# A hybrid DeltaNet and attention layer on one Trainium2 core: the products of levels 1 to 5 of the triangular inverse, one head at a time on half of the array

## The chip, the cores and the metric

One Trainium2 chip, one core of it. The metric is the device time of one execution, in microseconds (us). A result is the median of several executions, and a change is judged by the ratio of two kernels that ran on the same chip.

## The reference, cut to what matters

One residual layer over 4096 frames of width 1024. After an RMS norm and an input projection, two groups of heads work side by side: four heads of gated DeltaNet (head dimension 128, chunks of 64 frames) and eight query heads of sliding-window attention. Both are gated, concatenated and mapped by an output projection. The change lies in the DeltaNet part, in the solve of a unit lower triangular system for each head and chunk:

```python
lower = jnp.where(strict, jnp.einsum('bhnid,bhnjd->bhnij', k_beta, kc) * decay, 0.0)
eye = jnp.eye(CHUNK, dtype=jnp.float32)
rhs = jnp.concatenate([v_beta, k_beta * jnp.exp(G)[..., None]], axis=-1)
sol = lax.linalg.triangular_solve(eye + lower, rhs, left_side=True, lower=True, unit_diagonal=True)
```

The solved values feed a recurrence over the chunks, `v_new = val - kcu @ state`, from which output and next state follow.

## The kernel before, in words

The sequence is cut into 32 tiles of 128 frames. The kernel has 33 steps. Step `t` projects tile `t` and, in the same step, does all the work of the heads and the output projection for tile `m = t - 1`. The first step has only the projection, the last only the other part, and 31 steps have both. Each engine runs its own list of instructions, in the order in which `step` writes it, and the engines meet at semaphores (`done` waits for one).

PE's order is written out by hand (`step`, L383). The projection of tile `t` is cut into pieces, and `fill(n)` (L387) puts `n` of them between two parts of the other work, so that PE has something to do while DVE and ACT handle what the part before left. A piece is 24 or more matmuls in f16: lines L402 and L409. L597 is the output projection.

The inverse: the kernel solves for a tile of 128 frames at once. For each of the four heads it builds the inverse of a 128x128 unit triangular matrix by doubling. Level `lv` (1 to 6) joins diagonal blocks of size `2**lv` in pairs. With T the inverse so far, M the matrix, it takes P, the product of the odd rows' part of M with the even columns of T, keeps what belongs to the block pairs (a mask), and subtracts the product of the odd blocks of T with that from T. Only half of the columns of T and of M are touched at each level, 64 of each head's 128. The kernel keeps these halves packed: `t_even(lv)` and `t_odd(lv)` (L295, L298) are 128x256 each, 64 columns for each of the four heads, in one of two buffers `t_buf`; `m_odd` (L144) is the same for M, packed by POOL (`pack_m`, L1261).

A level from 1 to 5 has these parts:

- PE, `level_p` (L421): waits for T of the level before (`t_ready` from DVE, `t_moved` from ACT) and for `m_odd_ready`. It then multiplies pairs of heads: `m_odd` (128 columns, two heads) against `t_even` (128 columns, the same two heads), f32, into `bank[2]`, columns 0 to 255: line L432, two products. Each 128x128 result holds four 64x64 blocks, one pair of heads against itself and across. Then two transposes of `t_odd` into `bank[3]`, columns 0 to 255: line L436.
- DVE, `couple` (L947): reads both results, multiplies them by the level's mask and writes `below` (128x256): line L953, one operation of 256 columns. The mask of the level also clears the blocks across heads.
- ACT, `copy_u` (L694): copies the transposes to `u_odd` (L699), and `t_odd` to its place in the next level's packing (`next_columns(lv, 1)`, L700).
- PE, `level_t` (L447): waits for `p_ready` and `u_ready`, multiplies `u_odd` against `below` for the two pairs of heads, f32, into `bank[2]`, columns 256 to 511: line L452, two products.
- DVE, `update` (L956): subtracts the result from `t_even` and writes the next level's packing: line L958, one operation of 256 columns.

Level 6 is another form (L440, L444, L457): four products of 64 result rows, one for each head, and four transposes. Between the levels stand other parts of the step: the transposes of the softmax (L552), the attention's product with its values (L565: weights of 128 rows by 64 columns, results in turn on partitions 0 to 63 and 64 to 127), the product of keys and state (L417), and a fill. L531 is the attention's scores (weights of 64x64, on all four quarters of the array in turn), L518 four transposes ahead of the inverse. Of the work of a level, PE's order is: `level_p`, other parts or none, `fill(1)`, `level_t`, `fill(1)`. `level_p(4)` comes right after L565; ahead of every other `level_p` and `level_t` stands a fill, L409 for levels 1 to 3 and L402 for levels 4 (`level_t`) and 5.

On DVE the parts of the inverse stand between a convolution (L870, L872), the softmax (L1041, L1052), the gates and L1068, which scales the right-hand sides. The masks are made once, at the start: `mask_sym` from PE's transposes (L818), then five sums (L821).

Of the kernel before, what the change touches and what calls it, by code (L numbers as in the profile page):

```python
# [25 lines left out]
ALU = mybir.AluOpType  # L26
# [13 lines left out]
LEVELS = 7  # L40
# [34 lines left out]
def build(nc, x, pre_norm_w, w_in, conv_w, dn_a_log, dn_dt_bias, dn_out_norm_w, sw_sinks, w_out,  # L75
# [8 lines left out]
    with ExitStack() as ctx:  # L84
# [9 lines left out]
        bank = [ctx.enter_context(nc.psum_tensor(f"bank{i}", [128, 512], F32)) for i in range(8)]  # L94
# [45 lines left out]
        u_odd, below = flat[:, 0:256], flat[:, 768:1024]  # L140
        t_nat = work[:, 2:6, :]
        unread = prod.rearrange("p h n -> p (h n)").bitcast(mybir.dt.bfloat16)
        t_buf = [inv_t[:, :, :].rearrange("p h n -> p (h n)"), flat[:, 256:768]]
        m_odd = [cw[:, :, :].rearrange("p h n -> p (h n)")[:, 256 * i:256 * i + 256] for i in range(2)]  # L144
# [13 lines left out]
        masks = sb("masks", [128, LEVELS, 128], F16)  # L158
# [8 lines left out]
        def cut(at, n):  # L167
# [59 lines left out]
        p_turn, p_ready, tp_turn, t_turned, t_ready, u_ready, t_moved, m_odd_ready = (  # L227
            {lv: Nth(s, hi - lo + 1, lv - lo) for lv in range(lo, hi + 1)} for s, lo, hi in (
                (sem("p_turn"), 1, 6), (sem("p_ready"), 1, 6),
                (sem("tp_turn"), 1, 5), (sem("t_turned"), 1, 6), (sem("t_ready"), 1, 5),  # L230
                (sem("u_ready"), 1, 6), (sem("t_moved"), 1, 5), (sem("m_odd_ready"), 1, 5)))

        mask_turned, mask_link = sem("mask_turned"), sem("mask_link")
# [31 lines left out]
        def over_heads(ap, h):  # L265

            return ap.unsqueeze(1).broadcast_to([128, h, ap.shape[1]])
# [14 lines left out]
        def columns(flat_ap, lv):  # L282

            if lv == LEVELS - 2:
                return flat_ap.rearrange("p (q r) -> p q r", r=2 ** lv)
            return flat_ap.rearrange("p (q s r) -> p q s r", s=2, r=2 ** lv)

        def next_columns(lv, which):

            m = 2 ** lv  # L290
            if lv == LEVELS - 2:
                return t_nat.rearrange("p h (b s r) -> p (h b) s r", s=2, r=m)[:, :, which, :]
            return t_buf[lv % 2].rearrange("p (s q w r) -> p q s w r", s=2, w=2, r=m)[:, :, :, which, :]

        def t_even(lv):  # L295
            return t_buf[(lv - 1) % 2][:, 0:256]
# [4 lines left out]
        def heads(b):  # L301
            return bank[b][:, :].rearrange("p (h n) -> p h n", h=4)
# [58 lines left out]
        def _(pe):  # L361
            mm = nc.tensor.matmul
# [3 lines left out]
            for lv in range(LEVELS - 2):  # L366
                last = nc.tensor.transpose(mask_t[:, lv, :], masks[:, lv, :], ident16)
# [15 lines left out]
            def step(t, p, mix, proj, prep):  # L383
                m = t - 1
# [36 lines left out]
                def level_p(lv):  # L421

                    if lv == 1:
                        done(pe, t0_ready, m)
                    else:
                        done(pe, t_ready[lv - 1], m)
                        done(pe, t_moved[lv - 1], m)
                    if lv < LEVELS - 1:
                        done(pe, m_odd_ready[lv], m)
                        for g in range(2):  # L430
                            at = slice(128 * g, 128 * g + 128)
                            last = mm(bank[2][:, at], m_odd[lv % 2][:, at], t_even(lv)[:, at], start=True, stop=True)  # L432
                        last.then_inc(p_turn[lv].sem, 1)
                        for g in range(2):
                            at = slice(128 * g, 128 * g + 128)
                            last = nc.tensor.transpose(bank[3][:, at], t_odd(lv)[:, at], ident)  # L436
                        last.then_inc(t_turned[lv].sem, 1)
                        return
                    for h in range(4):
                        last = mm(bank[2][64:128, 64 * h:64 * h + 64], mt[:, h, 64:128], t_nat[:, h, 0:64],  # L440
                                  start=True, stop=True)
                    last.then_inc(p_turn[lv].sem, 1)
                    for h in range(4):
                        last = nc.tensor.transpose(heads(3)[:, h, :], t_nat[:, h, :], ident)  # L444
                    last.then_inc(t_turned[lv].sem, 1)

                def level_t(lv):  # L447
                    done(pe, p_ready[lv], m)
                    done(pe, u_ready[lv], m)
                    if lv < LEVELS - 1:  # L450
                        for g in range(2):
                            last = mm(bank[2][:, 256 + 128 * g:384 + 128 * g], u_odd[:, 128 * g:128 * g + 128],  # L452
                                      below[:, 128 * g:128 * g + 128], start=True, stop=True)
                        last.then_inc(tp_turn[lv].sem, 1)
                    else:
                        for h in range(4):
                            last = mm(bank[3][0:64, 64 * h:64 * h + 64], below[:, 64 * h:64 * h + 64],  # L457
                                      inv_u[:, h, 64:128], start=True, stop=True)
                        last.then_inc(up_turn, 1)
# [16 lines left out]
                for h in range(4):  # L476
                    last = nc.tensor.transpose(heads(2)[:, h, :], g_cols[:, h:h + 1].broadcast_to([128, 128]), ident)
# [5 lines left out]
                for h in range(4):  # L483
                    last = nc.tensor.transpose(heads(6)[:, h, :], k4[:, h, :], ident)
                last.then_inc(k_turned, 1)
                done(pe, qkv_ready[2], m)
                for h in range(4):
                    last = nc.tensor.transpose(heads(7)[:, h, :], v4[:, h, :], ident)
# [8 lines left out]
                for h in range(4):  # L497
                    last = nc.tensor.transpose(heads(3)[:, h, :], q4[:, h, :], ident)
# [314 lines left out]
        def _(dve):  # L813
# [5 lines left out]
            for lv in range(1, LEVELS - 1):  # L819
                dve.wait_ge(mask_link, lv)  # L820
                v.tensor_tensor(masks[:, lv, :], ident16 if lv == 1 else masks[:, lv - 1, :], mask_sym[:, lv - 1, :],  # L821
                                ALU.add).then_inc(mask_link, 1)
            v.memset(halo[:, :, :], 0.0)
            v.memset(state[:, :, :], 0.0)
            v.memset(v_win[:, :], 0.0)
# [117 lines left out]
            def step(t, p, mix, proj, prep):  # L943
# [3 lines left out]
                def couple(lv):  # L947

                    done(dve, p_turn[lv], m)
                    if lv == LEVELS - 1:  # L950
                        v.tensor_copy(below[64:128, :], bank[2][64:128, 0:256]).then_inc(p_ready[lv].sem, 1)
                        return
                    v.tensor_tensor(below.rearrange("p (g n) -> p g n", g=2), heads(2)[:, 0:2, :],  # L953
                                    over_heads(masks[:, lv, :], 2), ALU.mult).then_inc(p_ready[lv].sem, 1)

                def update(lv):  # L956
                    done(dve, tp_turn[lv], m)
                    v.tensor_tensor(next_columns(lv, 0), columns(t_even(lv), lv), columns(bank[2][:, 256:512], lv),  # L958
                                    ALU.subtract).then_inc(t_ready[lv].sem, 1)

                gate_steps = gates(t) if proj else None
                if mix:
# [424 lines left out]
```

## Time and profile before

| what | value |
|---|---|
| median of 3 runs | 2267.41 us (2266.87 to 2271.49) |
| profiled execution, first to last instruction (span) | 2265.5 us |
| median over that span | 1.9 us |
| PE, matmuls busy | 2144.3 us, 95%, 25798 records |
| PE, weight loads busy | 1836.1 us, 81% |
| DVE busy | 1672.2 us, 74% |
| ACT busy | 783.5 us, 35% |
| POOL busy | 653.2 us, 29% |

Of the profiled execution only the span is recorded, with no time of its own around it; the median of the runs stands 1.9 us over it, 0.08%.

How to read what follows. Times are us unless marked ns. L12 is line 12 of the kernel. PE is TensorE's matmuls, PEld its weight loads, which overlap them. An f32 product stands as two records: 160 levels (5 in each of 32 tiles) with two products each give L452 its x640. A group of the view by line reads: line, engine, operation, result<-operands, shapes, xcount | busy us, mean ns of one | idle us of the engine ahead of it, and who ended it. A shape of 128\*64 on PE is rows and columns of the weights, and the shape behind it the partitions and moving columns. The timeline and the chain read: start us, us, what, xcount; a run of like records is one row, from the start of the first to the end of the last. The ends of matmuls are modelled, and one stands some 0.2 us after its start while the next has long begun, so runs of different lines overlap in the timeline. The chain that ended last goes by steps from end to end, so its pieces add up. In the view by windows a row holds, for PE, PEld, DVE, ACT and POOL in turn, the busy us and in brackets the number of instructions (the window and its length stand ahead), then PE's granted clock as a share of full speed, the DMA share and GB/s.

### The profile page before, as it was taken

Reading aid. Unit: us, or ns where it says so; the run is one execution under the profiler, and the core shown is the slowest. Engines: PE = TensorE matmul, PEld = TensorE weight load, DVE = VectorE, ACT = ScalarE, POOL = GpSimd, SP = SyncE. Lnnn points to the kernel's source line nnn. Section 1 sums busy time; section 2 is a strip of 40 time slices with the busy share of each in tenths; the row PEclk is TensorE's granted clock in tenths of the full one; section 3 lists DMA queues with packets and bytes.
Section 4 is the critical chain, followed back from the end, with each engine's and each line's share of the span. In section 5 each row is a group of like instructions: output and inputs, shape, how many; then the busy total and the mean of one; then the engine's idle time right before and its main releaser. Section 6 shows DMA issues by size and latency. Waiting matters only on the chain.

```text
span 2265.5 us, 60918 instructions
## 1 busy us (share of the span) xinstructions
PE 2144.3 (95%) x25798; PEld 1836.1 (81%) x25798; DVE 1672.2 (74%) x4495; ACT 783.5 (35%) x2008; POOL 653.2 (29%) x875
## 2 busy tenths in 40 slices
PE   0389999999999999999999999999999999999996
PEld 0278888888888888888888888888888888888874
DVE  5887777777777777777777777777777777777764
ACT  0533333333333333333333333333333333333332
POOL 0022323332323332232333223233323233322322
PEclk9999999999999999999999999999999999999998
DMA  7101000000000000000000000000000000000000
GB/s 296 57 21 31 9 24 31 31 31 31 31 2 31 31 31 31 31 22 10 31 31 31 31 31 10 23 31 31 31 31 31 2 31 31 31 31 31 21 2 28
DMA packets 26321, 75.17 MB, mean 33 GB/s; under 512 B 5130, under 2 KB 9539, under 8 KB 25027
## 3 DMA queue, kind: packets, MB, share of 16 engines
q1 hardware_dynamic: 26050, 71.29, 9.0%
q8 instruction: 204, 3.34, 0.6%
q14 instruction: 67, 0.54, 0.1%
HBM read 54.50 MB, written 16.78 MB: 31 GB/s over the span
## 4 chain that ended last, share of the span: by engine, by line
PE 92%; DVE 5%; DMA 1%; ACT 1%; issue 1%; SPq 0%; POOL 0%; POOLq 0%; DVEq 0%; ACTq 0%
PE bank L402 37%; PE bank L597 14%; PE bank L409 11%; PE bank L417 9%; PE bank L432 3%; PE bank L452 3%; PE bank L436 2%; PE bank L565 1%; PE bank L531 1%; DVE w_raw L1209 1%; PE bank L552 1%; PE bank L380 1%; PE bank L440 1%; PE bank L457 1%; PE bank L444 1%; DVE small L1168 1%
## 5 line engine op out<-in xcount | busy, mean ns | idle before, releaser
L402 PE MATMUL bank<-xt_half,w_raw 128*128 128x128 f16 x15360 | 931.0, 219 | 54.8 <-DVE w_raw L1209 54.3
L402 PEld LDWEIGHTS bank<-xt_half,w_raw 128*128 128x128 f16 x15360 | 894.1, 98 | 62.1 <-DVE w_raw L1209 54.5
L872 DVE SCALAR_TENSOR_TENSOR qkv<-conv_in,cols,qkv 128x128 f32<-128x128 f32 x1152 | 431.2, 416 | 3.5
L409 PE MATMUL bank<-w_raw,xt_half 128*128 128x264 f16 (+1 forms) x1536 | 283.0, 328 | 0.0
L1266 POOL TENSOR_TENSOR cw<-mt,small 128x256 f32<-128x256 f32 x160 | 114.8, 726 | 369.8 <-PE bank L432 348.7
L409 PEld LDWEIGHTS bank<-w_raw,xt_half 128*128 128x128 f16 x1536 | 147.9, 98 | 77.7 <-issue 5.3
L699 ACT ACTIVATE work<-bank 128x256 f32<-128x256 f32 x160 | 61.5, 384 | 395.8 <-PE bank L436 395.8
L597 PE MATMUL bank<-w_o,inv_t 128*128 128x512 f16 x768 | 171.0, 379 | 2.1 <-DVE inv_t L1142 2.1
L597 PE MATMUL bank<-w_o,out_b_half 128*128 128x512 f16 x768 | 171.0, 379 | 0.0
L664 ACT ACTIVATE tanh_c<-qkv 128x512 f32<-128x512 f32 x96 | 60.5, 630 | 272.3 <-DVE qkv L872 272.3
L597 PEld LDWEIGHTS bank<-w_o,inv_t 128*128 128x128 f16 x768 | 73.8, 98 | 85.4 <-DVE inv_t L1142 2.4
L597 PEld LDWEIGHTS bank<-w_o,out_b_half 128*128 128x128 f16 x768 | 73.8, 98 | 83.1
L1314 POOL TENSOR_TENSOR small<-small 128x1 f32<-128x1 f32 x32 | 6.2, 194 | 435.2 <-ACT work L794 435.2
L953 DVE TENSOR_TENSOR work<-bank,masks 128x256 f32<-128x256 f32 x160 | 66.3, 414 | 86.1 <-PE bank L432 86.1
L1308 POOL TENSOR_TENSOR small<-small 128x4 f32<-128x4 f32 x32 | 33.9, 1058 | 275.3 <-DVE small L1125 275.3
L887 DVE SCALAR_TENSOR_TENSOR w_raw<-tanh_z,bank 128x512 f32<-128x512 f32 x64 | 43.8, 684 | 89.8 <-ACT tanh_z L673 89.8
L452 PE MATMUL bank<-work 128*128 128x128 f32 x640 | 101.4, 281 | 2.6 <-DVE work L953 1.5
L452 PEld LDWEIGHTS bank<-work 128*128 128x128 f32 x640 | 89.4, 192 | 12.6 <-DVE work L953 3.2
L1137 DVE TENSOR_TENSOR bank<-bank,w_raw 128x512 f32<-128x512 f32 x32 | 22.4, 700 | 99.1 <-PE bank L611 99.1
L870 DVE TENSOR_SCALAR qkv<-conv_in,cols 128x128 f32<-128x128 f32 x384 | 90.7, 281 | 5.1 <-ACT halo L657 1.6
L881 DVE SCALAR_TENSOR_TENSOR qkv<-tanh_c,qkv 128x512 f32<-128x512 f32 x96 | 66.1, 689 | 32.0 <-ACT tanh_c L664 32.0
L1324 POOL TENSOR_TENSOR y_out<-y_out,shared 128x1024 f32<-128x1024 f32 x32 | 75.4, 2357 | 30.7 <-DVE shared L1159 30.7
(219 smaller groups left out, 3727.6 us busy)
## 6 DMA issues: line engine op xcount, KB each, us to landing
x_in<-in_x_dram SPq DMA_DIRECT2D x32, 512.0 KB, 4.3
y_out<-in_x_dram SPq DMA_DIRECT2D x32, 512.0 KB, 3.9
out_dram<-y_out SPq DMA_DIRECT2D x32, 512.0 KB, 2.9
w_raw<-in_w_in_dram SPq DMA_DIRECT2D x8, 1024.0 KB, 12.6
w_o<-in_w_out_dram SPq DMA_DIRECT2D x8, 512.0 KB, 13.1
w_raw<-in_w_in_dram SPq DMA_DIRECT2D x8, 384.0 KB, 11.5
w_raw<-in_w_in_dram SPq DMA_DIRECT2D x8, 256.0 KB, 12.5
rot_tab<-in_rotary_dram SPq DMA_DIRECT2D x32, 64.0 KB, 4.0
```

What stands on the lines that cost most here:

```text
L402: last = mm(dst[:, 128 * b:128 * b + 128], w_half[:, c, ws, col:col + 128], xt_half[:, xs, c, :], start=(c == 0 and ws + xs == 0), stop=(c ...
L409: last = mm(dst[:, 0:n_col], xt_half[:, xs, c, :], w_half[:, c, ws, col:col + n_col], start=(c == 0 and ws + xs == 0), stop=(c == NC - 1 a ...
L417: last = mm(bank[b][:, 128 * h:128 * h + 128], lhs[:, h, :], right[:, h, :] if len(right.shape) == 3 else right, start=start, stop=stop)
L432: last = mm(bank[2][:, at], m_odd[lv % 2][:, at], t_even(lv)[:, at], start=True, stop=True)
L452: last = mm(bank[2][:, 256 + 128 * g:384 + 128 * g], u_odd[:, 128 * g:128 * g + 128], below[:, 128 * g:128 * g + 128], start=True, stop=True)
L597: last = mm(bank[4 + n][:, :], src[:, xs, i, :], w_out_half(c)[:, ws, 512 * n:512 * n + 512], start=(begin and i == 0 and xs + ws == 0), s ...
L870: last = v.tensor_scalar(dst, conv_in[:, b, 0:TOK], tap, None, ALU.mult)
L872: last = v.scalar_tensor_tensor(dst, conv_in[:, b, i:i + TOK], tap, dst, ALU.mult, ALU.add)
L881: v.scalar_tensor_tensor(y, tanh_c[:, :], 1.0, y, ALU.add, ALU.mult).then_inc(qkv_ready[g], 1)
L953: v.tensor_tensor(below.rearrange("p (g n) -> p g n", g=2), heads(2)[:, 0:2, :], over_heads(masks[:, lv, :], 2), ALU.mult).then_inc(p_read ...
L1266: g.tensor_tensor(m_odd[lv % 2].rearrange("p (q r) -> p q r", r=2 ** lv), rows_below, one.broadcast_to([128, 256]).rearrange("p (q r) -> p ...
L1324: g.tensor_tensor(y_out[:, :], y_out[:, :], shared[:, :], ALU.add).then_inc(post_ready, 1)
```

## The change

At levels 1 to 5 the packed layout stays, but the two products for pairs of heads become four, one for each head, and each uses half of the array.

- `level_p`: for head `h`, weights `m_odd` of the head, 128 rows by 64 columns, against its 64 columns of `t_even`. The result goes to partitions 0 to 63 for even heads and 64 to 127 for odd ones, columns 64 x (h // 2) of `bank[2]`. No block across heads is computed any more.
- `couple`: reads and writes 128 columns instead of 256. Its mask is the sum of the old mask's two halves, made once at the start by one more DVE operation.
- `level_t`: for head `h`, contraction over its 64 partitions: weights `u_odd`, 64 rows by 128 columns, against 64 columns of `below`. Even heads go to `bank[2]`, odd heads to `bank[3]`, columns 256 to 383.
- `update`: four operations of 64 columns, one for each head, instead of one of 256. `next_columns` takes a head for that.

The transposes, the copies on ACT, the packing on POOL, level 6, and the order of the parts are the same.

```diff
@@ next_columns
-        def next_columns(lv, which):
+        def next_columns(lv, which, head=None):
 
             m = 2 ** lv
+            one_of = slice(0, 4) if head is None else slice(head, head + 1)
             if lv == LEVELS - 2:
-                return t_nat.rearrange("p h (b s r) -> p (h b) s r", s=2, r=m)[:, :, which, :]
-            return t_buf[lv % 2].rearrange("p (s q w r) -> p q s w r", s=2, w=2, r=m)[:, :, :, which, :]
+                return t_nat[:, one_of, :].rearrange("p h (b s r) -> p (h b) s r", s=2, r=m)[:, :, which, :]
+            v = t_buf[lv % 2].rearrange("p (s h n) -> p s h n", s=2, h=4)[:, :, one_of, :]
+            return v.rearrange("p s h (q w r) -> p (h q) s w r", w=2, r=m)[:, :, :, which, :]
@@ level_p
-                        for g in range(2):
-                            at = slice(128 * g, 128 * g + 128)
-                            last = mm(bank[2][:, at], m_odd[lv % 2][:, at], t_even(lv)[:, at], start=True, stop=True)
+                        for h in range(4):
+                            at, side = slice(64 * h, 64 * h + 64), slice(64 * (h % 2), 64 * (h % 2) + 64)
+                            last = mm(bank[2][side, 64 * (h // 2):64 * (h // 2) + 64], m_odd[lv % 2][:, at],
+                                      t_even(lv)[:, at], start=True, stop=True)
@@ level_t
-                        for g in range(2):
-                            last = mm(bank[2][:, 256 + 128 * g:384 + 128 * g], u_odd[:, 128 * g:128 * g + 128],
-                                      below[:, 128 * g:128 * g + 128], start=True, stop=True)
+                        for h in range(4):
+                            g, side = h // 2, slice(64 * (h % 2), 64 * (h % 2) + 64)
+                            last = mm(bank[2 + h % 2][:, 256 + 64 * g:320 + 64 * g],
+                                      u_odd[side, 128 * g:128 * g + 128], below[side, 64 * g:64 * g + 64],
+                                      start=True, stop=True)
@@ masks, at the start
+            dve.wait_ge(mask_link, LEVELS - 1)
+            v.tensor_tensor(masks[:, 1:LEVELS - 1, 0:64], masks[:, 1:LEVELS - 1, 0:64],
+                            masks[:, 1:LEVELS - 1, 64:128], ALU.add)
@@ couple
-                    v.tensor_tensor(below.rearrange("p (g n) -> p g n", g=2), heads(2)[:, 0:2, :],
-                                    over_heads(masks[:, lv, :], 2), ALU.mult).then_inc(p_ready[lv].sem, 1)
+                    v.tensor_tensor(below[:, 0:128].rearrange("p (g n) -> p g n", g=2),
+                                    bank[2][:, 0:128].rearrange("p (g n) -> p g n", g=2),
+                                    over_heads(masks[:, lv, 0:64], 2), ALU.mult).then_inc(p_ready[lv].sem, 1)
@@ update
-                    v.tensor_tensor(next_columns(lv, 0), columns(t_even(lv), lv), columns(bank[2][:, 256:512], lv),
-                                    ALU.subtract).then_inc(t_ready[lv].sem, 1)
+                    for h in range(4):
+                        g, side, at = h // 2, h % 2, slice(64 * h, 64 * h + 64)
+                        last = v.tensor_tensor(next_columns(lv, 0, h), columns(t_even(lv)[:, at], lv),
+                                               columns(bank[2 + side][:, 256 + 64 * g:320 + 64 * g], lv), ALU.subtract)
+                    last.then_inc(t_ready[lv].sem, 1)
```

## Rows read from the trace of the kernel before

**Rows 1.** The page, the chain that ended last: shares of the span by engine.
```profile
PE 92%; DVE 5%; DMA 1%; ACT 1%; issue 1%; SPq 0%; POOL 0%; POOLq 0%; DVEq 0%; ACTq 0%
```

**Rows 2.** Busy time by windows, one window of the middle, 300 to 1200 us.
```profile
300.00:1200.00 900.00, 900.00 (x10903) 772.94 (x10902) 669.48 (x1869) 315.39 (x836) 276.15 (x368) 1.00 0.08 25
```

**Rows 3.** The chain in one step: start us, us, engine and line, count.
```profile
1020.44 0.44 PE bank L518 x4
...
1022.22 1.03 PE bank L531 x32
...
1026.73 0.44 PE bank L452 x4
...
1033.06 0.45 PE bank L432 x4
...
1037.67 1.02 PE bank L565 x16
1038.69 0.64 PE bank L432 x4
...
1039.56 1.34 PE bank L402 x24
1040.89 0.50 PE bank L452 x4
...
1042.73 0.50 PE bank L432 x4
...
1046.63 0.61 PE bank L440 x8
1047.24 0.59 PE bank L444 x4
...
1049.17 0.61 PE bank L457 x8
1049.78 1.45 PE bank L402 x24
```

**Rows 4.** Timeline of PE, the product of level 6: start us, us, line.
```profile
1046.56 0.68 PE L440 MATMUL bank<-work,mt 128*64 128x64 f32 x8
```

**Rows 5.** Line L440: duration of a record in ns, min/median/max.
```profile
L440 PE MATMUL bank<-work,mt x256: 222/222/270, 180.5 to 2236.2; 128*64 128x64 f32 x128
```

**Rows 6.** Groups by line, weight loads: busy us, mean ns of one.
```profile
L452 PEld LDWEIGHTS bank<-work 128*128 128x128 f32 x640 | 89.4, 192 | 12.6 <-DVE work L953 3.2
...
L531 PEld LDWEIGHTS bank<-k_win,q_rot 64*64 64x64 f32 x1024 | 27.6, 132 | 3.5 <-ACT k_win L725 0.2
...
L457 PEld LDWEIGHTS bank<-work 128*64 128x64 f32 x256 | 17.3, 137 | 4.2 <-DVE work L951 1.0
```

**Rows 7.** Groups by line, DVE: busy us, mean ns of one.
```profile
L953 DVE TENSOR_TENSOR work<-bank,masks 128x256 f32<-128x256 f32 x160 | 66.3, 414 | 86.1 <-PE bank L432 86.1
...
L1041 DVE TENSOR_TENSOR shared<-bank,small 128x512 f32<-128x512 f32 x64 | 41.0, 682 | 0.0
```

**Rows 8.** Timeline of DVE and of PE's loads, where t and p wait.
```profile
1027.21 0.42 DVE L958 TENSOR_TENSOR work<-inv_t,bank 128x256 f32<-128x256 f32 x1
...
1035.01 0.41 DVE L953 TENSOR_TENSOR work<-bank,masks 128x256 f32<-128x256 f32 x1
1035.35 1.11 DVE L1068 SCALAR_TENSOR_TENSOR rhs<-bank,small,rhs 128x128 f32<-128x128 f32 x4
...
1028.09 0.63 PEld L432 LDWEIGHTS bank<-work,cw 128*128 128x128 f32 x4
...
1035.51 0.63 PEld L452 LDWEIGHTS bank<-work 128*128 128x128 f32 x4
```

**Rows 9.** Timeline of the last step, one p.
```profile
2233.07 0.71 PE L432 MATMUL bank<-inv_t,cw 128*128 128x128 f32 x4 [0.51 <-DVE inv_t L958]
```

**Rows 10.** Timeline of DVE at the start, after the mask operations.
```profile
23.00 3.63 DVE L1168 TENSOR_REDUCE small<-w_raw 128x1 f32<-128x3336 f32 x1 [0.67 <-DMA w_raw<-in_w_in_dram]
```

## The prediction

> **What bounds the kernel now.** I read the chain that ended last first: TensorE holds 92% of it [rows 1]. Then one long stretch by windows: from 300 to 1200 us PE is busy for the whole 900 us at a granted clock of 1.00, VectorE for 669 of them [rows 2]. So in 31 of the 32 steps that hold the inverse, nothing makes PE wait, and a step takes as long as PE's stream of matmuls. Only what the change does to that stream counts, as long as the other engines stay hidden. Then the chain inside one such step, piece by piece [rows 3]. The reader is to see what a group of products costs there: L452 (two products of 128x128x128 in f32, in four records) takes 0.44 us behind L409 and 0.50 behind L402; L432, the same shape, 0.45 and 0.50. Products on part of the array stand in these rows too: L531 (64x64), L565 and L440, L457 (all 128x64), each with a price for going in and coming out.
>
> I call L432's group of a level p and L452's group t. Each is five times in a step.
>
> **The price of a tile shape.** L440 has eight records (four products, 64 moving columns). Its row in the timeline is 0.68 us long and one record 0.22 [rows 4, 5], so first start to last start is 0.46. The chain gives it 0.61 [rows 3]: 0.15 lie before its first record, where a record of L402 needs 0.056 (1.34/24). Going in costs 0.09. Coming out costs too: L444's four transposes take 0.59 in the chain, L518's four, with no such neighbour, 0.44: 0.15 more. After L457 the fill takes 1.45 for 1.34, 0.11 more. After L565 the next L432 takes 0.64 for 0.44, 0.20 more [rows 3]. An excursion of L440's kind is 0.61 + 0.15 = 0.76 and one of L457's 0.61 + 0.11 = 0.72.
>
> What runs side by side: L565 alternates between the halves and takes 1.02 us for sixteen records of 128 moving columns, 0.064 each against 0.11 for L452; L531, on four quarters, 1.03 for 32, 0.032 each [rows 3]. So tiles side by side do run at once. L440 keeps to one half: its 0.46 are 0.05 for the first weight load, which nothing covers, and seven steps of 0.058.
>
> **p, after.** Four products in place of two, eight records in four side-by-side pairs. First to last: 0.05 + 3 x 0.058 + 0.01 = 0.23 in place of L440's 0.46. The group is 0.76 - 0.46 + 0.23 = 0.53. Levels 1, 2 and 3 had 0.44: +0.09 each. Level 5 had 0.50: +0.03. Level 4 follows L565, which has the same tile shape: it goes in free, and L565's way out (0.20) moves behind it. Before: 0.64. After: 4 x 0.058 = 0.23 and 0.15 out, 0.38: -0.26. Sum of p: 0.27 + 0.03 - 0.26 = +0.04 us a step.
>
> **t, after.** Contraction over 64 rows, weights of 128 columns, 64 moving columns: no row has this shape. The question is the weight load. Loads of 64x64 take 132 ns, of 128x64 137, of 128x128 192 [rows 6]: they go with the columns, and not with the rows. The 128-column f32 load is about 0.11: behind L402 a group takes 0.50 and not 0.44, since a fill record of 0.056 hides only half of it [rows 3]. Eight records in four pairs then go by the load: 0.11 + 3 x 0.11 = 0.44 from first to last, and the 64 moving columns (0.058) save nothing. The group is 0.72 - 0.46 + 0.44 = 0.70. Levels 1 to 3 had 0.44 (+0.26 each), levels 4 and 5 had 0.50 (+0.20 each): +1.18. The Trainium skill has the rule by which I choose (TensorE: Matmul & The Clock Gate, LDWEIGHTS): a load lasts as its columns, whatever the contraction; an estimate from its figure, 128/1.2 = 107 ns, gives the same sum. That it holds for 64x128 no run here shows. The bounds: if the half array loads twice as fast, a pair takes 0.058 and t is 0.72 - 0.23 = 0.49 (+0.05 three times, -0.01 twice: +0.13 a step); if two halves of rows can't be loaded at once, eight loads follow each other, 0.88, and t is 1.14 (+0.70 three times, +0.64 twice: +3.38). I take 0.70: L531 shows different rows and columns loading at once, which the upper end denies, and the row of 64x64 against 128x64 speaks against the lower.
>
> **Couple and update on DVE.** TENSOR_TENSOR takes 414 ns at 256 columns and 682 at 512 [rows 7]: 1.05 ns a column, so 0.28 at 128 and 0.21 at 64. An operation of 0.41 holds the engine 0.34 (L953 at 1035.01, L1068 at 1035.35 [rows 8]), so one of 64 columns holds it 0.13 to 0.14. Couple: one of 128 in place of 256, -0.13. Update: four of 64 columns in place of one of 256, 4 x 0.135 - 0.34 = +0.20. Cost to the time: none, under PE. What covers it: the update of level 1 ends at 1027.63 and p's first load is at 1028.09, 0.46 spare; level 3's couple ends 1035.42 and t's load is at 1035.51, 0.09 spare [rows 8]. The latter is the tightest place. There DVE comes 0.20 - 0.13 = 0.07 later after t of level 2 ends, but PE meets t's way out (0.11), p's +0.09, a way in (0.09), and can no longer load ahead: more time than DVE adds. ACT copies the same 256 columns as before, POOL's packing waits for the same p: nothing.
>
> **The step without fills.** The last of the 32 steps has no fills, and there PE waits for DVE (0.51 before a p [rows 9]), so DVE's +0.07 a level and PE's way in and out come open: five levels of some 0.1, +0.5 us. **Mask sum at the start**: one DVE operation of 320 columns, by the same slope 0.5 us at most. DVE waits 0.67 for a weight DMA before its next large piece at 23.00 [rows 10]: hidden, 0; without that cover 0.5.
>
> **Sum.** 31 x (0.04 + 1.18) = 37.8, and 0.5: +38 us. Against the profiled execution's span, 2265.5, that gives 2304; the median of the runs is 2267.4, 1.9 over that span, so 2305.5 us.
>
> **Rivals.**
> Light loads: t at 0.49. 31 x (0.04 + 0.13) + 0.5 = +6: 2273. For it: half the moving columns and two halves at once. Against it: the load rows.
> Serial loads in t: 31 x 3.42 + 0.5 = +106: 2374. For it: no row shows two loads of 128 columns into halves. Against it: L531.
> DVE late: if an operation of 64 columns holds DVE 0.26, as one of 128 does, an update takes +0.70 and level 3's couple comes 0.57 later, past the 0.09 spare and PE's 0.3 to 0.5. Some 0.3 us a step in all, with t as forecast: +47, 2315. Against it: the slope of two sizes [rows 7].
> Faster: rows of the array are divided without going in and out, and loads go at half time. Then t is 0.23 + 0.06 = 0.29 (-0.15 three times, -0.21 twice: -0.87), the step -0.83, and -26 in all: 2242. It decides once the mean of t, 0.466 now, falls under 0.458 (p's +0.04 shared over five). For it: L531, L565 and L440, which show the price, all divide columns; none divides rows alone. Against it: it needs both. The skill's page TensorEngine Tiling (Array Packing), Theoretical Speedup, gives up to 2x where a dimension is at most 64; by that alone p and t would halve, 31 x 5 x 0.46 = -71, 2196. The rows of the trace disagree: L440, with half the columns on both sides, takes more than L452 and not less. The same page, Key Properties, says that a change of tiling mode drains the engine; the 0.09 and 0.15 agree.
> That the change doesn't do what it says has no room here: shapes and positions stand in the calls.
>
> **Chances.** Forecast (t near 0.70) 0.64; light loads 0.12; serial 0.08; DVE late 0.08; faster 0.08. A measurement of this kernel can tell about 0.2%, 4.5 us, from no change. Light loads straddle that: half to "same". Faster 0.08, same 0.06, slower 0.86. The range runs from just under the light case, 2270, to 2335, which holds the forecast with t up to 0.90 and the late DVE; the serial and the faster case, 0.16, stay out.
>
> **What would show it.** The two lines with twice the records, 1280 each. In the chain, p near 0.53 with the transposes behind it, level 4's p with no gap before it, t at 0.59 with 0.11 on the fill behind. Right: PE still busy for all of a window from 300 to 1200, DVE a little busier, each step 1.2 us longer. Wrong: t's first to last start in its timeline row near 0.23 or 0.88, a fill after t that takes 1.34, or waits of p and t for update or couple in the middle steps.

## The result, and the profile after

| | before | after |
|---|---|---|
| median of the runs | 2267.57 us (4 runs) | 2307.49 us (4 runs) |
| span of the profiled execution | 2265.5 us | 2305.1 us |
| PE busy, records | 2144.3 us, 25798 | 2185.1 us, 27078 |
| DVE busy, instructions | 1672.2 us, 4495 | 1656.7 us, 4976 |

The changed kernel is slower: ratio 1.0176, 95% interval 1.0161 to 1.0191. The forecast was 2305.5 us, and slower with a chance of 0.86; 2307.5 lies in the range. Two executions far outside all others, 2536 us of the kernel before and 4999 us of the update alone, are left out of the ratios.

PE is still the bound. In the same long window of the middle as [rows 2] it is busy throughout at full clock, and DVE is busy for 651 us of it where it was busy for 669. The row is from the view by windows.

```profile
300.00:1200.00 900.00, 900.00 (x11235) 743.59 (x11233) 651.39 (x2045) 309.75 (x825) 271.42 (x362) 1.00 0.08 26
```

A step can be measured from the first record of the attention's scores to the first one of a later step. The timeline of PE, before (L531) and after (L536), ten steps apart each time:

```profile
1022.15 1.10 PE L531 MATMUL bank<-k_win,q_rot 64*64 64x128 f32 x32
1688.35 0.99 PE L531 MATMUL bank<-k_win,q_rot 64*64 64x128 f32 x28
```

```profile
1037.69 1.10 PE L536 MATMUL bank<-k_win,q_rot 64*64 64x128 f32 x32
1715.82 0.99 PE L536 MATMUL bank<-k_win,q_rot 64*64 64x128 f32 x28
```

666.20/10 = 66.62 us before, 678.13/10 = 67.81 after: +1.19 us a step, 37.0 us in 31 steps, of the 39.6 by which the span grew. The rest comes in the last step, below. All step lengths in the next section are taken in this way.

The chain inside one step of the changed kernel. L434 is p (eight records now), L439 the transposes, L456 is t, L411 and L404 are the fills (L409 and L402 before), L570 the attention product. Two lines of the chain before, one pair of transposes (L436) and the fill behind a t (L409), go ahead for comparison.

```profile
1025.16 0.22 PE bank L436 x2
...
1027.17 1.29 PE bank L409 x6
```

```profile
1038.79 1.46 PE bank L411 x12
1040.25 0.38 PE bank L434 x8
1040.63 0.37 PE bank L439 x2
1041.00 1.35 PE bank L411 x12
1042.35 0.59 PE bank L456 x8
1042.94 1.40 PE bank L411 x6
...
1047.28 0.59 PE bank L456 x8
1047.87 1.40 PE bank L411 x6
...
1050.90 1.29 PE bank L411 x6
...
1054.23 1.02 PE bank L570 x16
1055.25 0.23 PE bank L434 x8
1055.48 0.37 PE bank L439 x2
1055.85 1.34 PE bank L404 x24
1057.19 0.59 PE bank L456 x8
1057.78 1.45 PE bank L404 x24
1059.23 0.38 PE bank L434 x8
```

The reader is to see three things, against [rows 3]. First, p is shorter than before, 0.38 for 0.44 or 0.50, but the two transposes behind it went from 0.22 to 0.37: together 0.75 for 0.66 at levels 1 to 3, and for 0.72 at level 5. Second, t is longer in itself, 0.59, and the fill behind it too, 1.40 for 1.29 and 1.45 for 1.34: 0.70 for 0.44 or 0.50. Third, p of level 4, right behind L570, takes 0.23, where L432 took 0.64, and the transposes behind it again cost 0.15 more: 0.60 for 0.86.

Weight loads by line, and the operations of DVE by line:

```profile
L456 PEld LDWEIGHTS bank<-work 64*128 64x128 f32 x1280 | 83.9, 186 | 43.0 <-issue 33.4 <-DVE work L961 3.2
...
L434 PEld LDWEIGHTS bank<-inv_t,cw 128*64 128x64 f32 x768 | 30.1, 136 | 25.0 <-issue 20.0 <-DVE inv_t L969 1.7
```

```profile
L969 DVE TENSOR_TENSOR work<-inv_t,bank 128x64 f32<-128x64 f32 x384 | 58.9, 215 | 49.1 <-PE bank L456 46.7
L961 DVE TENSOR_TENSOR work<-bank,masks 128x128 f32<-128x128 f32 x160 | 45.0, 281 | 63.2 <-PE bank L434 63.2
```

A load of 64 rows by 128 columns takes 186 ns, near the 192 of 128x128 and not near the 132 of 64x64 or the 137 of 128x64 [rows 6]: the columns count. An operation of 64 columns takes 215 ns on DVE and one of 128 281, where 0.21 and 0.28 were forecast.

### The profile page after: what moved, and what is told of

Same layout as the page of the kernel before. It is cut to its first block, busy times and chain, and to the rows that moved or that the text cites. A ratio compares the mean times of both kernels' runs of the same rounds, so it can differ in the third digit from the quotient of the medians.

```text
span 2305.1 us, 63959 instructions
## 1 busy us (share of the span) xinstructions
PE 2185.1 (95%) x27078; PEld 1805.8 (78%) x27078; DVE 1656.7 (72%) x4976; ACT 782.8 (34%) x2008; POOL 648.5 (28%) x875
## 4 chain that ended last, share of the span: by engine, by line
PE 92%; DVE 5%; DMA 1%; ACT 1%; issue 0%; SPq 0%; POOLq 0%; POOL 0%; DVEq 0%; ACTq 0%
PE bank L404 37%; PE bank L602 14%; PE bank L411 11%; PE bank L419 9%; PE bank L456 4%; PE bank L439 3%; PE bank L434 2%; PE bank L570 1%; PE bank L536 1%; DVE w_raw L1221 1%; PE bank L557 1%; PE bank L382 1%; PE bank L443 1%; PE bank L462 1%; PE bank L447 1%; DVE small L1180 1%
## 5 line engine op out<-in xcount | busy, mean ns | idle before, releaser
L404 PE MATMUL bank<-xt_half,w_raw 128*128 128x128 f16 x15360 | 932.7, 219 | 54.4 <-DVE w_raw L1221 53.9
L404 PEld LDWEIGHTS bank<-xt_half,w_raw 128*128 128x128 f16 x15360 | 887.1, 98 | 67.0 <-DVE w_raw L1221 54.1
L880 DVE SCALAR_TENSOR_TENSOR qkv<-conv_in,cols,qkv 128x128 f32<-128x128 f32 x1152 | 397.4, 387 | 3.5
L411 PE MATMUL bank<-w_raw,xt_half 128*128 128x264 f16 (+1 forms) x1536 | 283.7, 328 | 0.0
L411 PEld LDWEIGHTS bank<-w_raw,xt_half 128*128 128x128 f16 x1536 | 142.7, 98 | 81.2 <-issue 5.3
L456 PEld LDWEIGHTS bank<-work 64*128 64x128 f32 x1280 | 83.9, 186 | 43.0 <-issue 33.4
L1320 POOL TENSOR_TENSOR small<-small 128x4 f32<-128x4 f32 x32 | 33.8, 1057 | 278.4 <-DVE small L1137 278.4
L456 PE MATMUL bank<-work 64*128 64x64 f32 x1280 | 105.9, 284 | 2.5 <-DVE work L961 1.4
L969 DVE TENSOR_TENSOR inv_t<-work,bank 128x64 f32<-128x64 f32 x256 | 39.2, 215 | 76.8 <-PE bank L456 76.8
L969 DVE TENSOR_TENSOR work<-inv_t,bank 128x64 f32<-128x64 f32 x384 | 58.9, 215 | 49.1 <-PE bank L456 46.7
L961 DVE TENSOR_TENSOR work<-bank,masks 128x128 f32<-128x128 f32 x160 | 45.0, 281 | 63.2 <-PE bank L434 63.2
```

Of the source, the lines that this page charges most:

```text
L404: last = mm(dst[:, 128 * b:128 * b + 128], w_half[:, c, ws, col:col + 128], xt_half[:, xs, c, :], start=(c == 0 and ws + xs == 0), stop=(c ...
L411: last = mm(dst[:, 0:n_col], xt_half[:, xs, c, :], w_half[:, c, ws, col:col + n_col], start=(c == 0 and ws + xs == 0), stop=(c == NC - 1 a ...
L456: last = mm(bank[2 + h % 2][:, 256 + 64 * g:320 + 64 * g], u_odd[side, 128 * g:128 * g + 128], below[side, 64 * g:64 * g + 64], start=True ...
L880: last = v.scalar_tensor_tensor(dst, conv_in[:, b, i:i + TOK], tap, dst, ALU.mult, ALU.add)
L969: last = v.tensor_tensor(next_columns(lv, 0, h), columns(t_even(lv)[:, at], lv), columns(bank[2 + side][:, 256 + 64 * g:320 + 64 * g], lv) ...
```

## The experiments

The theory, A: a change of tile shape costs PE 0.09 us going in and 0.11 to 0.15 coming out, halves and quarters side by side do run at once, weight loads go by their columns, and DVE and ACT are hidden. The rivals: B, DVE's update in four parts is the cost; C, t pays for its number of records, or for its moving columns on top of its loads. The ratios are against the kernel before on the same chip.

**The first product alone.** `level_p` with halves; its results go where the pair products put theirs, so couple, t and update are those of before.

```diff
-                        for g in range(2):
-                            at = slice(128 * g, 128 * g + 128)
-                            last = mm(bank[2][:, at], m_odd[lv % 2][:, at], t_even(lv)[:, at], start=True, stop=True)
+                        for h in range(4):
+                            at, side = slice(64 * h, 64 * h + 64), slice(64 * (h % 2), 64 * (h % 2) + 64)
+                            last = mm(bank[2][side, at], m_odd[lv % 2][:, at], t_even(lv)[:, at], start=True, stop=True)
```

> Only the first product of a level is changed (four on the halves of the array), the second and DVE's operations are as before. Theory A (shape changes cost PE 0.09 us going in and 0.11 to 0.15 coming out, and are the whole effect): levels 1 to 3 +0.09 us each, level 5 +0.03, level 4 -0.26, together +0.04 us a step, +1 us in all, 2268 to 2269 us. Theory B (the slowdown comes from DVE's four-part update, shapes are neutral): p stays at 0.44 in the chain, and the time is that of before, 2267.5.

Measured: 2268.9 us, ratio 0.9996 (0.9987 to 1.0005); a step 66.66, +0.04. The time alone can't tell A from B here, but the chain can: L432 is now at 0.38 with 0.37 for the transposes at levels 1, 2, 3 and 5, and at 0.23 at level 4. So the halves gain and lose in different places, and the sum is almost nothing.

**The second product alone.** p and couple as before, t and update as changed; t reads `below[side, 64 * h:64 * h + 64]`.

> The first product and couple as before, the second product and the update as changed. A: levels 1 to 3 +0.26 us each, 4 and 5 +0.20, together +1.18 a step, 31 steps: +36.6 and one or two us in the last step, 2305 to 2307 us. With the first-product kernel at its +1 that adds up to the whole change. If the two parts hid each other's costs instead, the sum would fall short by several us. A second theory of the sum: where t is slow, p's way in is partly paid by it; then this one alone would come out over 2310.

Measured: 2310.1 us, ratio 1.0177 (1.0160 to 1.0194); a step 67.78, +1.16. With the first product's +0.04 that is +1.20, and the whole change has +1.19: the parts add up. The median lies over the 2305 to 2307 of A, and also just over the 2310 that the second theory asked for, though the step does not. The surplus is in the last step: from its first record of the scores to the end it is 55.4 us here, 49.7 before and 52.3 in the changed kernel, and the granted clock was lower (0.75 over the last 65.5 us, 0.91 before). So the few us over the sum are no second mechanism of p and t.

**The update alone.** The kernel before with `update` as four operations of 64 columns (`next_columns` takes a head here as in the change, which the cut leaves out):

```diff
-                    v.tensor_tensor(next_columns(lv, 0), columns(t_even(lv), lv), columns(bank[2][:, 256:512], lv),
-                                    ALU.subtract).then_inc(t_ready[lv].sem, 1)
+                    for h in range(4):
+                        at = slice(64 * h, 64 * h + 64)
+                        last = v.tensor_tensor(next_columns(lv, 0, h), columns(t_even(lv)[:, at], lv),
+                                               columns(bank[2][:, 256 + 64 * h:320 + 64 * h], lv), ALU.subtract)
+                    last.then_inc(t_ready[lv].sem, 1)
```

> The kernel before with nothing changed but the update, four operations of 64 columns in place of one of 256. A: DVE is hidden under PE in 31 steps: +0 to +1.5 us, all of it in the last step. B: most of the 40 us, 2295 us or more, with PE waiting for the update in the middle steps. Between them: the tightest place before had 0.09 us to spare at level 3 and this adds 0.2 to it, with none of the slower PE stream to cover it; if that shows, 0.1 us a step, +3 us.

Measured: ratio 1.0008 (0.9997 to 1.0018); a step 66.62, to the last digit that of before. B falls, and in the steps not even the in-between case shows. The median, 2273.7 us, lies 4.7 over that of the kernel before on this chip, which A's +0 to +1.5 does not cover. Six of its nine executions took 2272.0 to 2274.1 us and three 2267.7 to 2268.2; the kernel before has both groups too, 7 of 24 from 2271.8 to 2273.9. The profiled execution is of the longer group: its last step, from the scores to the end, took 55.2 us for 49.7, at a granted clock of 0.77 for 0.91 over the last 65.5 us. Whether four operations make that group more frequent stays open. DVE's timeline around level 3, with the row of POOL that runs beside it:

```profile
1032.71 0.61 DVE L962 TENSOR_TENSOR inv_t<-work,bank 128x64 f32<-128x64 f32 x4 [0.59 <-PE bank L454]
1033.24 2.15 DVE L874 SCALAR_TENSOR_TENSOR qkv<-conv_in,cols,qkv 128x128 f32<-128x128 f32 x4
1035.31 0.41 DVE L908 TENSOR_TENSOR small<-small 128x4 f32<-128x4 f32 x1
...
1032.20 1.90 POOL L1290 TENSOR_TENSOR shared<-shared,small 128x1024 f32<-128x1024 f32 x1 [1.68 <-DVE small L1063]
```

The update holds DVE for 0.53 (1032.71 to 1033.24), as forecast. The four convolution operations behind it took 2.15 us; in the kernel before the same four took 2.34:

```profile
1032.13 2.34 DVE L872 SCALAR_TENSOR_TENSOR qkv<-conv_in,cols,qkv 128x128 f32<-128x128 f32 x4
...
1031.29 1.90 POOL L1285 TENSOR_TENSOR shared<-shared,small 128x1024 f32<-128x1024 f32 x1 [1.68 <-DVE small L1058]
```

They gave the 0.2 back, and the couple of level 3 was no later than before. The records of the trace, one by one, show why: only the first of the four is long, 1.20 us before and 1.00 here, and in both kernels it ends 0.15 us after POOL's operation (1033.18 before, 1034.10 here). The update's extra 0.2 falls into a time in which DVE stood still for POOL anyway.

**Level 4 alone.** The same edit as the first experiment's, at `lv == 4` only, all else as before.

> Only the first product of level 4 is changed, which stands right behind the attention product of the same tile shape. A: that product goes in free and takes the way out over from its neighbour, -0.26 us a step, -8 us in all: 2259.5 us, faster than both kernels. B: no difference from before.

Measured: 2260.0 us, ratio 0.9961 (0.9948 to 0.9973); a step 66.36, -0.26, as forecast. It is faster than both kernels. The chain behind the attention product (L568 here, p is L435):

```profile
1034.14 1.02 PE bank L568 x16
1035.17 0.23 PE bank L435 x8
1035.40 0.37 PE bank L439 x2
1035.77 1.34 PE bank L402 x24
```

**The same, with the transposes between.** In `level_p(4)` the two transposes go ahead of the four products. The same instructions run, in another order. The cut is against the kernel with level 4 alone.

```diff
+                        if lv == 4:
+                            for g in range(2):
+                                at = slice(128 * g, 128 * g + 128)
+                                last = nc.tensor.transpose(bank[3][:, at], t_odd(lv)[:, at], ident)
+                            last.then_inc(t_turned[lv].sem, 1)
...
                         last.then_inc(p_turn[lv].sem, 1)
-                        for g in range(2):
-                            at = slice(128 * g, 128 * g + 128)
-                            last = nc.tensor.transpose(bank[3][:, at], t_odd(lv)[:, at], ident)
-                        last.then_inc(t_turned[lv].sem, 1)
+                        if lv != 4:
+                            for g in range(2):
+                                at = slice(128 * g, 128 * g + 128)
+                                last = nc.tensor.transpose(bank[3][:, at], t_odd(lv)[:, at], ident)
+                            last.then_inc(t_turned[lv].sem, 1)
```

> The kernel with the halves at level 4 alone, and there the two transposes ahead of the four products, so that they stand between the attention product and the products of the same tile shape. Same instructions, other order. A (the gain of level 4 is the change of shape that the neighbours share): transposes 0.22 + 0.15, products 0.38, fill behind +0.11: 0.86 from the attention product to the fill in place of 0.60, +0.26 a step, +8 us, back at before: 2268 us. If the gain is in the products themselves: 2260 us again.

Measured: 2269.0 us, ratio 0.9993 (0.9984 to 1.0002); a step 66.62. The whole gain is gone with nothing changed but what stands next to what:

```profile
1038.38 1.02 PE bank L574 x16
1039.41 0.37 PE bank L433 x2
1039.78 0.38 PE bank L440 x8
1040.16 1.45 PE bank L402 x24
```

L433 are the transposes, L440 the products. 0.37 + 0.38 + 0.11 on the fill (1.45 for 1.34) = 0.86, for 0.23 + 0.37 = 0.60. This is the cleanest sign that the price belongs to the border between two tile shapes, and not to the products.

**The same, with the transposes first.** They stand ahead of the attention product, with a wait for `t_ready[3]` and `t_moved[3]` of their own.

> The same kernel with level 4's transposes ahead of the attention product. A: they cost 0.22 there, behind a fill, and the way out of the shape falls on f16 fill records (0.11) and no longer on f32 transposes (0.15): 0.56 in place of 0.60, -0.04 a step, -1.2 us against the kernel with level 4 alone, 2258.8 us; below what a measurement can tell, so to be read in the chain. It would be slower if the transposes now wait for the update of level 3.

Measured: 2260.7 us, ratio 0.9957 (0.9944 to 0.9971); a step 66.32, -0.04 against level 4 alone. In the chain:

```profile
1033.74 0.22 PE bank L566 x2
1033.97 1.02 PE bank L575 x16
1034.99 0.23 PE bank L435 x8
1035.22 1.45 PE bank L402 x24
```

0.22 + 0.23 + 0.11 = 0.56, as expected. The times of whole executions can't tell it from level 4 alone.

**One border more in each level.** The changed kernel with p cut in two: two products, one transpose, two products, one transpose.

```diff
-                        for h in range(4):
-                            at, side = slice(64 * h, 64 * h + 64), slice(64 * (h % 2), 64 * (h % 2) + 64)
...
-                        last.then_inc(p_turn[lv].sem, 1)
                         for g in range(2):
+                            for h in (2 * g, 2 * g + 1):
+                                at, side = slice(64 * h, 64 * h + 64), slice(64 * (h % 2), 64 * (h % 2) + 64)
...
+                            if g:
+                                last.then_inc(p_turn[lv].sem, 1)
                             at = slice(128 * g, 128 * g + 128)
                             last = nc.tensor.transpose(bank[3][:, at], t_odd(lv)[:, at], ident)
```

> The changed kernel with the first product's group split: two products, one transpose, two products, one transpose. Same work, one more change of shape there and back in each level. A: a further way in 0.09, first load in the open 0.05, way out 0.15: +0.29 in 155 places, +45 us, 2352 us. If changes of shape cost nothing in themselves and the prices in the trace belong to the groups next to them: no change.

Measured: 2357.4 us, ratio 1.0387 (1.0372 to 1.0403); a step 69.31, +1.49 against the changed kernel, 0.30 for each of five levels. The price of going out and in, first load included, was expected at 0.29 and shows with no product added.

**t on quarters.** The changed kernel, each second product split into two of 64x64 weights.

```diff
-                            last = mm(bank[2 + h % 2][:, 256 + 64 * g:320 + 64 * g],
-                                      u_odd[side, 128 * g:128 * g + 128], below[side, 64 * g:64 * g + 64],
-                                      start=True, stop=True)
+                            for o in (0, 64):
+                                last = mm(bank[2 + h % 2][o:o + 64, 256 + 64 * g:320 + 64 * g],
+                                          u_odd[side, 128 * g + o:128 * g + o + 64],
+                                          below[side, 64 * g:64 * g + 64], start=True, stop=True)
```

> The changed kernel, with the second product on quarters of the array: eight products of 64x64 weights in place of four of 64x128, same result. A (weight loads last as their columns, and tiles side by side load at once): t is 0.05 + 3 x 0.058 inside and 0.51 in all in place of 0.70, -0.19 in 155 places, -29 us against the changed kernel: 2278 us. C (t pays for its number of records, or the rows can't load at once): 16 records in place of 8 cost as much or more, 2307 us or more, up to 2370.

Measured: 2276.1 us, ratio 1.0029 (1.0019 to 1.0039); a step 66.81, -1.00 against the changed kernel. Twice the instructions, and faster. The chain (t is L457 here):

```profile
1029.19 0.39 PE bank L457 x16
1029.58 1.40 PE bank L411 x6
```

0.39 for 0.59, with the fill behind it unchanged at 1.40: what went is the load of 128 columns in each pair. C's count of records falls. The kernel is still 0.3% slower than the one before, since the borders are still paid.

**t with 128 moving columns.** The changed kernel, t against `below[side, 0:128]`, results 128 columns apart; the added columns are not read.

> The changed kernel, each of the four second products with 128 moving columns in place of 64 (the added ones are not read). A (t goes by the load of 128 weight columns, 0.11 a pair, and the 64 moving columns of 0.06 hide under it): 128 moving columns need 0.107 a pair and still hide, save the last pair's end, +0.05 in each of 155 places at most, 2307 to 2315 us. C (t goes by moving columns plus load, one after the other): +0.05 for each of four pairs, +0.2 in 155 places, +31 us, 2338 us.

Measured: 2315.9 us, ratio 1.0204 (1.0189 to 1.0220); a step 68.08, +0.27, 0.053 for each t. Twice the moving columns cost one pair's end and not four: the 0.11 of the load covers them. The median lies just over the 2315 that A gave at most, while the step's +0.27 is the +0.05 for each t that A allowed. C's other form, +0.2 for each t, falls.

**p in another order.** The changed kernel with `for h in (0, 2, 1, 3)` in `level_p`, so that two products of one half follow each other.

> The changed kernel, the first products in the order of heads 0, 2, 1, 3: two on the lower half one after the other, then two on the upper. A1 (products run side by side only where neighbours in the list lie on different halves): the inside of p goes from 0.23 towards L440's 0.46, of the four pairs one or none is left, +0.1 to +0.2 in 155 places, +15 to +31 us. A2 (PE picks from a longer stretch of the list): no change, 2307.5 us.

Measured: 2310.5 us, ratio 1.0182 (1.0166 to 1.0197); a step 67.89, +0.08. p is 0.39 for 0.38, and 0.28 for 0.23 at level 4: much nearer to A2. The halves need not alternate in the list for PE to run them side by side; the order costs 0.01, and 0.05 where p follows the attention product.

## Why the prediction was right, point by point

**The bound.** PE's stream set the time before and sets it after; that DVE and ACT stay hidden was the condition. Between 200 and 2190 us no profile of this study has a wait of PE, and the update alone has tested the part that was in doubt.

**p.** Forecast: 0.53 with the way out, +0.09 three times, +0.03, and -0.26 at level 4; in sum +0.04 a step. Measured: 0.38 and 0.15 on the transposes, 0.53; 0.23 and 0.15 at level 4; the first product alone gives +0.04 a step. Mechanism and size were right.

**t.** Forecast: 0.59 and 0.11 on the fill. Measured: 0.59 and 0.11, and +1.16 a step for +1.18. The choice between 0.11 and 0.058 for a pair carried most of the sum: had I taken the lower end, the forecast would have been 2273. The rule of the Trainium skill that stood beside it (TensorE: Matmul & The Clock Gate, LDWEIGHTS: a load lasts as its columns) now has its row for 64x128. The trace agrees that columns count and rows don't; the record itself lasts 186 ns, and what comes near the 107 ns of the estimate is the step from pair to pair, 0.105 us. Inside t two details were off by as much in opposite ways, and that their sum came out is luck:

```profile
1042.28 0.66 PE L456 MATMUL bank<-work 64*128 64x64 f32 x8
1042.87 1.47 PE L411 MATMUL bank<-w_raw,xt_half 128*128 128x512 f16 x6
```

```profile
1049.10 0.68 PE L457 MATMUL bank<-work 128*64 128x64 f32 x8
1049.71 1.46 PE L402 MATMUL bank<-xt_half,w_raw 128*128 128x128 f16 x23
```

With records of 0.27, t of level 1 after (first two lines) has 0.39 from first to last start and not 0.44, since the first load in the open added 0.05 and not 0.11. From its last start to the fill there are 0.20 us, where L457 before (last two lines, records of 0.22) has 0.15. So the way out of t is the dearer one by 0.05; why stays open.

**DVE.** Length and holding time of the short operations were right. "DVE a little busier" was wrong: it is busy 15.5 us less, with 481 more instructions. The update did add time, but the scalar_tensor_tensor of the convolution went from a mean of 416 ns to 387 over 1152 instructions, 33.8 us less, because it stood still for POOL for less time (the last section). This cost and gained nothing, since PE is the bound. The mask sum at the start was hidden: the first record of the scores starts at 156.12 us, at 156.10 before.

**The last step.** The term that failed: forecast +0.5 us, measured +2.6 (39.6 - 37.0). Most of it isn't the change's work but the clock. In its last part PE ran the same 32 records of the state products, before in 4.0 us and after in 6.3. The view by windows over them, before and then after:

```profile
2238.90:2243.00 4.10, 4.00 (x33) 3.84 (x34) 1.39 (x3) 0.00 (x0) 0.00 (x0) 1.00 0.00 0
```

```profile
2276.00:2282.60 6.60, 6.36 (x33) 6.29 (x34) 1.52 (x3) 0.00 (x0) 0.00 (x0) 0.58 0.00 0
```

A mean of 0.58 is the lower level, 1.2 GHz, for most of the window; before, the whole window had 2.4 GHz. Ahead of it, in both, PE had stood still again and again for DVE, ACT and POOL (0.2 to 1.5 us at a time, once 3.4). Before, the lower level fell elsewhere in the step and caught less work, so part of it was already paid: L565 took 1.61 us there and L570 1.09 after. The last step's clock differs between kernels whose last steps are nearly alike, over the last 65.5 us from 0.75 to 0.91 in the profiles of this study, and the stretch from the last scores to the end took 48.3 (first product alone) to 55.4 us (second product alone, and the split). So up to some 6 us against the kernel before can come from it in a single execution. Whether the change pushes it one way wasn't tried.

**The sum.** 31 steps gave 37.0 us where 37.8 were forecast, the last step 2.6 where 0.5 were: the span grew by 39.6, forecast 38.3. That the total came out within 2 us is in part luck, since the last step moves by more than that from one profile to another.

**The rivals.** Light loads: a pair of t's loads took 0.11, not 0.058. Serial loads: pairs do load at once, 0.11 for two records. DVE late: no wait of p or t for DVE in the middle steps, in any kernel. Faster: a product that divides only the rows does have a way in (0.09) and out (0.11), like the other shapes. The Trainium skill's factor of up to 2 (TensorEngine Tiling (Array Packing), Theoretical Speedup) shows in p at level 4, 0.23 for the 0.44 of a p without borders, and was eaten by the borders at the other levels; it did not show in t. The prediction's argument against it, that L440 takes more than L452, does not bear on it, since L440's products all lie on one half.

## What to carry to other kernels

A matmul on part of the array must save more than the two borders that it puts into PE's stream, here 0.25 to 0.3 us, so group what has the same tile shape: one p given the shape of its neighbour gained 0.4%, and all ten groups of a step, nine of them behind full-size matmuls, cost 1.8%. Before splitting over the contraction, look at what the weight load takes: with few moving columns it sets the pace, and quarters (64 columns) beat halves (128) here, by 0.20 us a group. Where one engine holds the whole chain, price its stream from neighbouring rows, group by group; a neighbour's longer row is part of the price.

## What the runs showed of the hardware that was not expected

- PE pairs products on different halves even when the list has two of the same half in a row: 0.39 for 0.38.
- DVE's scalar_tensor_tensor of the convolution stands still while some operations of POOL run. Record by record, 742 of the 1152 before had no operation of POOL beside them and took 345 ns on the mean, the other 410 took 545; after, 804 took 344 ns and 348 took 485. At level 3 the one that starts during POOL's 1.90 us operation ends 0.15 us after it in all three kernels looked at (1.20 us long before, 1.00 in the update alone, 0.57 in the changed kernel). It isn't the speed of POOL: its packing went from 726 to 699 ns in the changed kernel, but with the second product alone it took 729 while the convolution's mean fell to 392 all the same. So what stands ahead of an operation on DVE can be free, when it falls into such a wait.
- The granted clock of the last step (0.75 to 0.91 over 65.5 us) goes with an end that comes up to some 6 us later or earlier, from one profile to another, and executions of the kernel before on one chip spread as far (2267.2 to 2273.9 us). The smallest effects sought here are no larger. The step's length in the middle, from two rows of the timeline, told 0.04 us a step apart.
